# Hybrid encoder layer: the condition vector's halves kept in PSUM, turned probabilities in the scores' bank, out-projection begun among the heads

## What is computed

```python
mod = silu(c) @ w_ada + b_ada                       # 6 vectors of 2048
sh_a, sc_a, g_a, sh_m, sc_m, g_m = split(mod, 6)
h = rms_norm(x, norm_mix) * (1 + sc_a) + sh_a
p = h @ w_in                                        # 512 + 256 + 64 + 3*512 + 3*512 + 8 columns
q  = rms_norm(p_cq, q_norm) @ w_uq                  # 8 latent heads, 128 + 64 (rotary)
kv = rms_norm(p_ckv, kv_norm) @ w_ukv               # keys 128, values 128 per head
o = concat(head_norm(latent attention),             # 8 heads of 128, softmax, chunk mask
           head_norm(stick-breaking attention),     # 8 heads of 64
           head_norm(forgetting attention))         # 8 heads of 64, softmax
x = x + g_a * (o @ w_out)
h = rms_norm(x, norm_ffn) * (1 + sc_m) + sh_m
x = x + g_m * (relu(h @ w_ff1) ** 2 @ w_ff2)
return rms_norm(x, final_norm)
```

## Time and profile before

| | us |
|---|---|
| median of 3 runs | 1243.65 |
| lowest, highest | 1239.12, 1246.18 |
| the profiled execution | 1246.57 |
| its span | 1244.8 |
| PE busy | 1154.9 (93%) |
| DVE busy | 775.3 (62%) |
| ACT busy | 520.8 (42%) |
| POOL busy | 321.4 (26%) |
| read from HBM | 293.37 MB, 237 GB/s over the span |

### The profile page before, as it was taken

The page is one execution under the profiler, slowest core; times in us unless marked ns, Lnnn a source line. Parts: engine busy times, 40 slices in busy tenths (PEclk is TensorE's granted clock), DMA queues, the critical chain, the costliest instruction groups (busy, mean ns, idle before and its releaser), DMA issues.

```text
span 1244.8 us, 21630 instructions
## 1 busy us (share of the span) xinstructions
PE 1154.9 (93%) x9066; PEld 1115.6 (90%) x9066; DVE 775.3 (62%) x952; ACT 520.8 (42%) x628; POOL 321.4 (26%) x139
## 2 busy tenths in 40 slices
PE   4989999687897996899999999999999999999996
PEld 3879988676667995899999999999999999999995
DVE  4597678984898456877777544444555555455454
ACT  3533453444343433444444433333444444344341
POOL 2776889576402983000000000000000000000000
PEclk8989999887897998899999999999999999999998
DMA  8899899654884799478878555565555655655551
GB/s 337 305 390 365 342 352 335 236 220 184 305 273 152 272 366 358 141 268 291 285 260 264 187 187 186 186 187 187 185 188 184 190 186 183 192 187 179 194 182 68
DMA packets 81311, 296.87 MB, mean 238 GB/s; under 512 B 9024, under 2 KB 9152, under 8 KB 81216
## 3 DMA queue, kind: packets, MB, share of 16 engines
q1 hardware_dynamic: 81216, 295.50, 68.4%
HBM read 293.37 MB, written 2.10 MB: 237 GB/s over the span
## 4 chain that ended last, share of the span: by engine, by line
PE 71%; DVE 9%; POOL 8%; DMA 6%; issue 4%; ACT 1%; SPq 0%; DVEq 0%; ACTq 0%; POOLq 0%
PE ps L1142 44%; PE ps L1148 22%; POOL w_lo L664 7%; DMA ada<-in_ada 4%; DVE ada L748 4%; DMA raw<-in_weights 2%; PE ps L1161 1%; PE ps L1198 1%; PE ps L1191 1%; DVE qk L815 0%; PE ps L1184 0%; DVE mx L946 0%; POOL ssq L658 0%; PE ps L1166 0%; PE ps L1244 0%
## 5 line engine op out<-in xcount | busy, mean ns | idle before, releaser
L388 ACT ACTIVATE w_hi<-raw 128x1024 fp32r<-128x1024 f32 x362 | 381.2, 1059 | 522.5 <-PE ps L1148 388.8
L736 DVE TENSOR_TENSOR w_lo<-raw,w_hi 128x1024 fp32r<-128x1024 f32 x256 | 316.4, 1244 | 292.4 <-ACT w_hi L388 291.7
L1142 PE MATMUL ps<-hT,w_hi 128*128 128x256 f32 x3072 | 399.4, 282 | 28.4 <-DVE hT L856 13.4
L1142 PEld LDWEIGHTS ps<-hT,w_hi 128*128 128x128 f32 x3072 | 380.8, 190 | 32.4 <-issue 22.6
L664 POOL TENSOR_TENSOR w_lo<-raw,w_hi 128x1024 fp32r<-128x1024 f32 x106 | 273.3, 2604 | 87.7 <-ACT w_hi L388 87.3
L1142 PE MATMUL ps<-act,w_hi 128*128 128x256 f32 x2048 | 261.8, 279 | 0.0
L1142 PEld LDWEIGHTS ps<-act,w_hi 128*128 128x128 f32 x2048 | 250.1, 188 | 0.0
L1148 PE MATMUL ps<-hT,w_lo 128*128 128x256 f32 x1536 | 215.2, 282 | 1.1 <-POOL w_lo L664 1.1
L1148 PEld LDWEIGHTS ps<-hT,w_lo 128*128 128x128 f32 x1536 | 196.6, 190 | 2.5 <-POOL w_lo L664 2.5
L658 POOL TENSOR_TENSOR ssq<-ssq,sq 128x1024 f32<-128x1024 f32 x6 | 14.5, 2416 | 686.9 <-ACT sq L395 686.9
L1148 PE MATMUL ps<-act,w_lo 128*128 128x256 f32 x1024 | 141.4, 279 | 0.0
(11 more groups left out here) (191 smaller groups left out, 767.1 us busy)
## 6 DMA issues: line engine op xcount, KB each, us to landing
raw<-in_weights SPq DMA_DIRECT2D x362, 512.0 KB, 4.3
ada<-in_ada SPq DMA_DIRECT2D x192, 512.0 KB, 5.7
xT<-in_xt SPq DMA_DIRECT2D x4, 512.0 KB, 7.0
y<-tmp SPq DMA_DIRECT2D x2, 512.0 KB, 2.6
consts<-in_consts SPq DMA_DIRECT2D x1, 580.0 KB, 5.2
y<-sq SPq DMA_DIRECT2D x1, 512.0 KB, 2.6
y<-ssq SPq DMA_DIRECT2D x1, 512.0 KB, 2.6
cols<-in_cols SPq DMA_DIRECT2D x1, 219.5 KB, 2.6
```

The source lines that it names most:

```text
L388: sc.activation(w_hi[:, slot, :, :], raw[:, slot, :, :], ACT.Copy).then_inc(hi_done, 1)
L736: ve.tensor_tensor(w_lo[:, slot, :, :], raw[:, slot, :, :], w_hi[:, slot, :, :].bitcast(F32), ALU.subtract).then_inc(lo_vec, 1)
L1142: pe.matmul(acc[:, n, :], w, rhs[:, kt0 + k, half, :], start=first and k == 0 and n % 2 == 0 and half == 0, stop=False, skip_group_check=True)
```

## The change

Four things are changed.

**Condition tiles.** The 96 tiles from A_GA to A_GM come in another order: 24 tiles of the second half (16 of the attention gate, 8 of the shift) in the last part of the input projection, three a block; then 48 of the first half in the steps (20 at t < 8, 28 later); then the 24 remaining of the second half in the out-projection. All read the vector from PSUM. The sum of the half that comes first is kept in `part_sum`. The first half of the vector stays in ps0 banks 2 and 3 until the out-projection takes them; ACT copies only the second half back. The last 32 tiles, in the feed-forward, read `c_rep`.

**Banks and the latent stage.** The latent products all use ps0 banks 0 and 1, and each waits for ACT's read of the one before. Stick scores use ps1 banks 0 to 2. The first latent product stands ahead of the first scores. The queries are rotated at t = 7 by PE and t = 8 by DVE. The sums and the shared key's rotation in the last part get a bank pair of their own (`USE_LST`) and are read by DVE in one piece.

**Softmax heads.** Scores use ps1 banks 0 and 1 and ps0 bank 0, and the turned probabilities are written over the scores of the same head. The scores of head j wait for the copy of head j-3.

**Out-projection.** It uses ps0 banks 2, 3 and ps1 banks 0, 1 in turn. Blocks 0 and 1 are mixed so that their eight units of stick and forgetting heads come first, two of them at t = 24 and 25. The norm's multiplies are 16 instructions of one head and 128 tokens, and each pair of heads is turned when it is ready.

```diff
+OUT_BLOCK = (0, 0, 1, 1, 0, 0, 1, 1, 0, 0, 0, 0, 1, 1, 1, 1) + 8 * (2,) + 8 * (3,)
+OUT_K = (0, 1, 0, 1, 2, 3, 2, 3, 4, 5, 6, 7, 4, 5, 6, 7) + 2 * tuple(range(8))
...
-        return range(A_GA + 16 + 5 * t // 2, A_GA + 16 + 5 * (t + 1) // 2)
-    first = A_GA + 16 + 5 * H // 2
-    at = lambda i: first + 31 * min(18, i) // 18
+        return range(A_X + 5 * t // 2, A_X + 5 * (t + 1) // 2)
+    at = lambda i: A_X + 20 + 28 * min(17, i) // 17
...
+            if USE_OUT <= use < USE_FFN:
+                return (ps[0][:, 2:4, :], ps[1][:, 0:2, :])[(use - USE_OUT) % 2]
+            return ps[use % 2][:, 0:2, :]
...
+        latents = ps[0][:, 0:2, :]
...
-            return (ps[0][:, 2, :], ps[0][:, 3, :], ps[1][:, 2, :])[i % 3]
+            return ps[1][:, i % 3, :]
...
-            return (ps[0][:, 0, :], ps[0][:, 1, :], ps[0][:, 3, :])[j % 3]
-
-        def turn_bank(j):
-
-            return ps[1][:, j % 2, :]
+            return (ps[1][:, 0, :], ps[1][:, 1, :], ps[0][:, 0, :])[j % 3]
...
             for t in range(STEPS):
+                if 1 <= t < H:
+                    read_latent(t - 1)
                 if t < H:
                     soft_parts(t)
                 if 1 <= t < H:
-                    read_latent(t - 1)
                     for v in LAT_OF[t - 1]:
                         hi(B_LAT + LAG, 0, 0, v)
...
+                if t == H + 17:
+                    hi(B_OUT + LAG, 0, 0, 0)
+            out_hi(2)
+            hi(B_OUT + LAG, 0, 0, 1)
+            out_hi(3)
+            hi(B_OUT + LAG, 0, 0, 2)
             square_outputs(3)
+            hi(B_OUT + LAG, 0, 0, 3)
             head_rough(2, AT_ML, H)
...
-            for v in range(4, 6):
+            for v in range(4, 10):
                 lo(B_LAT + v)
             gp.wait_ge(latent_read, 3)
             gp.tensor_tensor(q_rope[:, :, :], rope_raw[:, :, :], cos4, ALU.mult).then_inc(rope_term, 1)
-            for v in range(6, 10):
+            for v in range(10, 10 + LAG):
                 lo(B_LAT + v)
...
+                ve.tensor_tensor_reduce(out=ada[:, slot, :], in0=ada[:, slot, :], scale=1.0,
+                                        scalar=part if second else bias, in1=c, op0=ALU.mult, op1=ALU.add,
+                                        accum_out=mod[:, g, kt:kt + 1] if second else part
...
-            for c in range(2):
+            for n in range(H):
                 for q in range(2):
-                    o = o_tok[:, q, c * BW:(c + 1) * BW].rearrange("p (h d) -> p h d", d=VD)
-                    at = AT_ML + 4 * c
-                    ve.tensor_tensor(o, o, hss[:, q, at:at + 4].unsqueeze(2).to_broadcast([P, 4, VD]),
-                                     ALU.mult).then_inc(normed_mla, 1)
+                    o = o_tok[:, q, n * VD:(n + 1) * VD]
+                    ins = ve.tensor_scalar(o, o, hss[:, q, AT_ML + n:AT_ML + n + 1], None, ALU.mult)
+                if n % 2 == 1:
+                    ins.then_inc(normed_mla, 1)
...
+                if n:
+                    pe.wait_ge(latent_read, n)
+                else:
+                    pe.wait_ge(psum_free, USE_OUT)
...
-                if j >= 3:
-                    pe.wait_ge(probs_ready, j - 2)
+                elif j == 2:
+                    pe.wait_ge(rope_turned, 1)
+                else:
+                    pe.wait_ge(probs_copied, j - 2)
...
+            for j in range(2, U_OUT):
+                if j in (7, 8):
+                    out_turn(2 * j - 10)
+                    out_turn(2 * j - 9)
+                out_unit(j)
```

278 lines of the change are left out of this document (147 added, 131 removed).

## The result

The changed kernel takes 1237.72 us (median of 19 runs, 1232.39 to 1241.54) against 1242.33 us (19 runs, 1238.50 to 1250.75): a ratio of 0.9948, 95% interval 0.9932 to 0.9964. The profiled execution has a span of 1232.9 us against 1244.8.

The account below looks back on a forecast made before the run. The feed-forward is PE alone and unchanged; the 320 us before it, where PE idles or runs slow, decide. 1 + 12.5 - 2.5 + 2 + 6 = 19 us off 1246.6 gives 1227.6, or 1225 us as median; range 1214 to 1237.

Parts of the forecast that it names:

- part 2: Stick heads: POOL's new order removes most PE waits, the single latent bank pair adds some; 12.5 us gained (8 to 14).
- part 4: Tail to out-projection unit 8: early units gain, small scaling operations meet POOL's subtractions; 2 us gained (6 lost to 7 gained).
- nothing of it lasts: Rival, whole kernel: POOL's wait just moves, or the load and small-operation rivals come together; 1240 us, chance 6%.
- three signs: Softmax step above 3.5 us, last input part ending later than 250, or PE waiting 3 us or more at each latent product.
- Part 1: Last input part: condition multiplies reading PSUM avoid waiting for POOL, but more tiles load; 1 us gained (5 gained to 5 lost).
- slower hand-over through ACT: Rival, stick heads: ACT's high parts wait for raw weights, seven latent products start 4 us late each; 1251 us, chance 6%.
- Part 3: Softmax heads: scores wait for the copy of turned probabilities three heads back; 2.5 us lost (0 to 6).
- my own bound from the row of 256 elements: Tail scaling: a 256-element operation took 2.48 us while POOL was busy, so small size doesn't protect it.
- Part 5: End of the out-projection: five fewer transfers let DVE's last gating start earlier; 6 us gained of at most 7.7 (lowest 2).

Follow-up runs that it names:

- e2: The changed kernel with part_sum allocated behind the last tensor, so every other tensor keeps its address from the kernel before; 1222.76 us, ratio 0.9836.
- e18: The kernel before with 128 unused bytes between half_sum and rstd, ahead of hT; 1215.22 us, ratio 0.9765.
- e17: Repeat of e13, the changed kernel with sums at the end and 128 unused bytes ahead of hT; 1194.06 us, ratio 0.9600.
- e15: e2 with the 24 condition multiplies of the last input part reading the vector from SBUF; 1205.20, 1232.35, 1234.40 and 1240.96 us.
- e16: e2 with only the 48 condition multiplies among the heads reading the vector from SBUF; 1258.17 us, ratio 1.0123.
- e9: The kernel before with only POOL's order of latent subtractions changed; 1230.30 and 1240.61 us once each, ten runs from 1249.03 to 1258.69.
- e8: e2 with the last heads scaled by 4 operations of 512 elements instead of 16 of 128; 1221.01 us, ratio 0.9834.
- e13: e2 with 128 unused bytes ahead of hT; 1195.39, 1196.56, 1196.20 and once 1224.36 us, ratio 0.9622.

## Why the prediction was wrong

By its own steps, against before's profile, for the changed kernel and for e2, which has before's addresses. A plus is time gained.

| step | predicted | changed | e2 |
|---|---|---|---|
| 1 last input part (last v_fx sum; 244.4 before) | +1 | -0.8 | +1.0 |
| 2 stick heads, to the first softmax scores | +12.5 | +17.7 | +15.2 |
| 3 softmax heads | -2.5 | -2.3 | -1.6 |
| 4 tail, last scores to unit 8 | +2 | +1.2 | +0.2 |
| out-projection, unit 8 to the last | 0 | -0.3 | +1.0 |
| 5 its border to the feed-forward | +6 | +9.7 | +6.7 |
| feed-forward and end | 0 | -13.4 | +0.7 |
| sum | 19 | 11.8 | 23.2 |

**The step that failed** is the sentence that the change touches the feed-forward "only by which copy of the condition vector 32 multiplies of DVE read". The change also touches it through the allocation. I read the diff for instructions, and took the new tensor for a place to keep sums. It shifts the moving operand of the 6144 matmuls of the feed-forward and costs 13.4 us, 70% of the sum. No rival had it, and the 20% left outside the range was for mishaps in the stages that I knew. Without the shift (e2) the time is 22.2 us below before, 1222.76, 2 us off the forecast, and at the quick address the change is worth 21.2 (e18 to e17). That it comes so near is partly luck, since part 2 gave 3 to 5 us more than forecast and part 4 up to 2 less. The measured 1237.7 also lies near the rival "nothing of it lasts" (1240), but not for its reason: 25 us were gained ahead of the feed-forward. And none of the three signs came by which I would have called myself wrong (a step above 3.5 us, the last part beyond 250, waits of 3 us at each latent product); all three looked at stages that I had thought about.

**Part 1** held in mechanism: no multiply before the out-projection is above 1.3 us on average. (The 24 in the last part took 30.1 us; my 29 had them at 1.2 us where the earlier trace rows has 1.28.) The SBUF — State Buffer page of the Trainium skill, section Who interferes with whom, was the ground for it; by e15 and e16, the runs agree, with 24 multiplies at 2.06 us again in e15 and 10.3 us more for the part. The part's end moves by some us from execution to execution (240.6 in e9 and 244.4 in before, with the same code), so the +1 can't be told from nothing. What I didn't see is what this operand protects: in e9 and e16, with DVE busy all the time at the border, PE had to wait there for POOL, and TensorE's clock fell in the softmax heads. Nothing in before's profile showed half-clock softmax heads, since there the clock was 1.00.

**Part 2** was undersized. The waits came as listed, in kind: one for POOL's first low part (7.8 us, where I took over 4.4: PE now reached it 3 us earlier), then 1.63 and 0.46 for ACT's reads, and nothing at the later products, for which I had 1.5 in all (and had counted five where there are four). DVE's copy cost nothing where I had 1.4. The clock was 0.91 rather than 0.82. Against my 62.2 us the stage took 57.5: the first latent product ended 9.7 us after the last input sum for 11, and the waits behind it were 2.6 us in all for 6.1. The term measured 15 to 18 where 14 was my upper end. The slower hand-over through ACT, my rival on the other side, was not there at all. e9 gives the cause: its 16.5 us came with POOL's order and two pairs of banks. So POOL's order makes the gain, and the single pair costs no more than these 2.1 us of waits.

**Part 3** was right: a step of 3.25 us for 3.2 to 3.3. **Part 4** was right: the scaling is 9.7 us long between the subtractions, the turns wait for it, unit 7 starts at +35.7 as forecast, and unit 8 at +41.1 (396.95 against the last scores at 355.9) where I had +40.4. Only PE's idle time ahead of the eighth unit, for which I had 3 to 6 us, was 1.08 (and 1.2 more ahead of the ninth); in e2 it was 3.28. That the Trainium skill (same section) lets tensor_scalar block and be blocked by GpSimd agrees with e2's row beside e8 (operations of 0.28 us of which the longest lasts 2.42), and so does my own bound from the row of 256 elements; the 16 small ones are neither better nor worse than the four.

**Part 5** had the right mechanism and too low a bound in the changed kernel: DVE's last gating starts 2.3 us behind PE's last unit (468.62 against 466.29), where 10.2 lay between them before, so 7.9; and the other 1.8 us are the residual sums themselves. Their eight matmuls took 3.78 us before, at a granted clock of 0.50, and 1.99 in the changed kernel, at 1.00, where PE had stood only 1.64 us ahead of them and not 9.56. I had taken what follows the gating as unchanged. In e2 (3.23 us of standing, 3.43 of sums) the part is 6.7, about as predicted.

## What to carry over

Read a diff for its allocations too: where PE is full, compare its matmuls in 100 us in a stretch that the change doesn't touch before arguing about the stretches that it does. When a kernel is bound by matmuls, try unused bytes ahead of the moving operand; here 128 of them and the sums at the end give 1194.06 us, 4.0% under before, of which the change itself is 1.7. Which offset is the quick one has to be measured, as the cause is not known. And a gain in one stage can be lost if the next one is reached with DVE and POOL behind and PE waiting: in e9 and e16 the clock then fell for much longer than the wait.

## What the runs showed of the hardware

- TensorE's pace in back-to-back matmuls of 256 columns (each weight tile loaded beside them, clock 1.00, PE never waiting by the profile) took the values 836, 845, 852, 855 and 885 in 100 us, so 119.6 to 113.0 ns, in programs that differ in nothing but SBUF addresses. The Trainium skill, TensorE: Matmul & The Clock Gate, section Back-to-back issue gap, has 262 cycles for 256 columns, for a matmul by itself and not in a stream with weight loads; at 2.4 GHz that makes 109.2 ns, an estimate, and no layout here reached it. The Trainium skill, SBUF — State Buffer, says in Who interferes with whom that PE never waits on anyone, with separate ports for moving operand and weights; the 6% measured between layouts speak against reading this as a pace that no layout changes.
- One program can have two such paces: e13 three times about 1196 us and once 1224, e18 five times about 1215 and once 1243.5, e15 once 1205 and three times 1232 to 1241. Differences of 26 to 30 us are what 852 in place of 885 makes of the products (6144 matmuls of the feed-forward by 4.4 ns are 27). The odd runs themselves have no profile.
- The softmax heads can run at 1.2 GHz for 53 us (e9) or 58 us (e16) with PE busy 53.00 and 57.42 us of it, and cost 26 us more then. The clock fell behind a wait of PE of 2.8 us (e9, with one of 1.2 ten us ahead of it) or 2.1 us (e16, with one of 6.8 some 17 us ahead of it). Behind the 6.8 us of e16 and the 4.4 us of before it fell too, but was back at 2.4 GHz after some 6 us. So neither the length of the wait nor a busy PE tells how long the clock stays down; what does is open.
- A DVE operation of 128 elements with one SBUF tensor took 0.28 us, or 2.4 us when it met a POOL subtraction of 2.4 us (e2); the 16 together took as long as four of 512 elements with two SBUF tensors (9.58 and 9.11 us).
